# One program per engine for the front, the attention and the mix of a Hyena and attention encoder layer

## What is computed

```python
xn = rms_norm(x, norm1); proj = xn @ w_in            # -> hyena x0, x1, v | q | k | v
y_hy = hyena_mixer(...)      # width-3 conv; x0 * (long_filter * (x1 * v)) + skip, by Fourier transform
y_at = window_gqa(...)       # 8 heads of 64, 2 key heads, |q-k| <= 128, bias table, sink logit
mixed = concat([rms_norm(y_hy, hy_gain), rms_norm(y_at, at_gain)])
h = x + mixed @ w_out
y = h + (silu(gate) * up) @ w_down                   # gate, up = rms_norm(h) @ w_gate_up
```

## Time and profile before

| | us |
|---|---|
| three runs: median (lowest to highest) | 3209.15 (3200.5 to 3214.08) |
| the profiled execution: its time, its span | 3206.01, 3204.3 |
| TensorE busy | 2984.3 (93%) |
| VectorE, ScalarE, GpSimd busy | 1652.3 (52%), 1037.4 (32%), 358.5 (11%) |
| granted TensorE clock, mean over the span | 0.961 |
| front, up to TensorE's last product | 0 to 918.8 |
| front's end, bias rows, first loads of attention | 918.8 to 963.1 |
| attention | 963.1 to 1214.5 |
| loads of the mix, then the mix | 1214.5 to 1454.3 |
| feed-forward (first instruction) | 1463.65 to the end |

### The profile page before, as it was taken

The page is one execution under the profiler, slowest core; times in us unless marked ns, Lnnn a source line. Parts: engine busy times, 40 slices in busy tenths (PEclk is TensorE's granted clock), DMA queues, the critical chain, the costliest instruction groups (busy, mean ns, idle before and its releaser), DMA issues.

```text
span 3204.3 us, 41415 instructions
## 1 busy us (share of the span) xinstructions
PE 2984.3 (93%) x15240; PEld 2686.5 (84%) x15240; DVE 1652.3 (52%) x2394; ACT 1037.4 (32%) x1754; POOL 358.5 (11%) x411
## 2 busy tenths in 40 slices
PE   5988999898969997995999999899999989999998
PEld 4877889788956775885999999799999979999997
DVE  6765767685646886553343343433343344343343
ACT  4443544454525773213111211321111222121111
POOL 4322111232103550000000000000000000000000
PEclk9999999999986998997999999899999999999999
DMA  5466867765932224443221211321221232221220
GB/s 150 159 213 181 248 200 245 228 195 160 234 124 68 79 66 153 122 122 126 79 66 52 79 52 53 118 80 53 79 65 52 65 118 72 60 65 52 79 65 39
DMA packets 328861, 361.85 MB, mean 113 GB/s; under 512 B 39854, under 2 KB 269102, under 8 KB 328215
## 3 DMA queue, kind: packets, MB, share of 16 engines
q1 hardware_dynamic: 291032, 264.54, 29.3%
q0 software_dynamic: 37728, 95.96, 8.8%
HBM read 264.09 MB, written 83.12 MB: 108 GB/s over the span
## 4 chain that ended last, share of the span: by engine, by line
PE 51%; DMA 1%; DVE 1%; ACT 0%; issue 0%; SPq 0%; POOL 0%; POOLq 0%; DVEq 0%; ACTq 0%
PE ff_acc L81 12%; PE ff_acc L82 12%; PE ff_acc L83 12%; PE ff_down L81 6%; PE ff_down L83 6%; PE ff_down L82 6%; DMA ff_h<-h_dram 0%; DMA y<-ff_h 0%; DVE ff_xlo L2298 0%; DVE ff_xs L2287 0%; DMA ff_raw<-w_gate_up 0%; PE ff_down L2187 0%; ACT ff_xs L2242 0%; ACT ff_xhi L2248 0%; DVE ff_prod L2308 0%
## 5 line engine op out<-in xcount | busy, mean ns | idle before, releaser
L81 PE MATMUL ff_acc<-ff_xhi,ff_whi 128*128 128x384 f32 x2112 | 711.3, 337 | 16.3 <-DVE ff_xlo L2298 15.2
L82 PE MATMUL ff_acc<-ff_xlo,ff_whi 128*128 128x384 f32 x2112 | 709.7, 336 | 0.0
L83 PE MATMUL ff_acc<-ff_xhi,ff_wlo 128*128 128x384 f32 x2112 | 709.6, 336 | 0.0
L81 PEld LDWEIGHTS ff_acc<-ff_xhi,ff_whi 128*128 128x128 f32 x2112 | 399.8, 189 | 19.7 <-issue 13.8
L82 PEld LDWEIGHTS ff_acc<-ff_xlo,ff_whi 128*128 128x128 f32 x2112 | 399.9, 189 | 1.2
L83 PEld LDWEIGHTS ff_acc<-ff_xhi,ff_wlo 128*128 128x128 f32 x2112 | 399.4, 189 | 0.0
L2319 DVE TENSOR_TENSOR ff_h<-ff_h,ff_down 128x512 f32<-128x512 f32 x396 | 270.5, 687 | 228.1 <-PE ff_down L83 228.1
L2308 DVE TENSOR_TENSOR ff_prod<-ff_silu,ff_acc 128x384 f32<-128x384 f32 x132 | 73.2, 554 | 600.5 <-ACT ff_silu L2259 600.5
L81 PE MATMUL ff_down<-ff_dhi,ff_ahi 128*128 128x512 f32 x792 | 309.1, 390 | 7.3 <-DVE ff_alo L2311 7.3
L83 PE MATMUL ff_down<-ff_dhi,ff_alo 128*128 128x512 f32 x792 | 309.2, 390 | 0.0
L82 PE MATMUL ff_down<-ff_dlo,ff_ahi 128*128 128x512 f32 x792 | 309.1, 390 | 0.0
(11 more groups left out here) (261 smaller groups left out, 4925.9 us busy)
## 6 DMA issues: line engine op xcount, KB each, us to landing
ff_raw<-w_gate_up SPq DMA_DIRECT2D x134, 512.0 KB, 5.1
ff_draw<-w_down SPq DMA_DIRECT2D x33, 1024.0 KB, 5.1
pr_raw<-w_in SPq DMA_DIRECT2D x108, 256.0 KB, 5.5
pr_xs<-x SPq DMA_DIRECT2D x36, 512.0 KB, 4.6
f_dram<-fi_out POOLq DMA_DIRECT2D x32, 512.0 KB, 4.1
fs_a<-f_dram SPq DMA_DIRECT2D x32, 512.0 KB, 6.5
mo_x_in<-x SPq DMA_DIRECT2D x18, 512.0 KB, 4.2
h_dram<-mo_h POOLq DMA_DIRECT2D x18, 512.0 KB, 6.2
```

Source lines behind the costliest of these rows:

```text
L81: pe.matmul(out, still[0], moving[0], start=start, stop=False)
L82: pe.matmul(out, still[0], moving[1], start=False, stop=False)
L83: return pe.matmul(out, still[1], moving[0], start=False, stop=stop)
```

## The change

`front`, `bias_rows`, `attend` and `mix_out` become `front` and `mixers`. Each returns five functions, one per engine, and `build` opens one block in which each engine runs its part of the front and then its part of the mixers. In place of the barrier every engine first goes through `finished`, which waits for the front's last events (all stores landed too).

Moved into the front: k's high and low parts and v's transposes and parts (one stage `kvst`, stored to `k2_dram` and `v2_dram`, 6 pieces each), and the bias rows, in the steps `z_step`. 40 semaphores of the front are cleared by GpSimd at `z_step(4)` and given to the mixers. The others are cleared at the end of the block: 132 in all.

In the mixers block n has the attention of query block n, the preparation (turn of y, gate, norms) of tile n-1 and the mix matmuls of tile n-2, so there are 20 blocks. All is unrolled. There are two score banks instead of four. The probabilities aren't divided any more: the inverse sums are spread out by GpSimd, transposed by TensorE (`turn_denominators`, one bank in turn with the units and y), copied by ScalarE and multiplied into the finished output by GpSimd. The biased scores wait for one maximum per four heads instead of one per head. The w_out slices are loaded with two buffers in blocks 0 and 1.

The core of the diff (new lines, in the order of the file):

```diff
+    def finished(engine):
...
+        engine.wait_ge(handed_on, 1)
+        engine.wait_ge(unit_done, 2 * first_unit(ROUNDS))
+        engine.wait_ge(inverse_done, N2)
+        engine.wait_ge(hyena_out, 2 * NU + 2 * CT * NG)
...
+    def heads_at(n, i):
...
+        return ((0, 1), (2,), (3,), (4, 5), (6,), (7,))[i] if units(n) == 6 else ((0, 1), (2, 3), (4, 5), (6, 7))[i]
+    def mix_steps(n, i):
...
+        bounds = (0, 3, 6, 8, 11, 14, 16) if units(n) == 6 else (0, 4, 8, 12, 16)
+        return range(bounds[i], bounds[i + 1])
...
+        def bank(free_sem, free_at):
...
+            n = len(uses)
+            if n >= 2:
+                pe.wait_ge(*uses[n - 2])
+            uses.append((free_sem, free_at))
+            return n % 2
...
+            if 8 * n + h >= 2:
+                pe.wait_ge(biased, 8 * n + h - 1)
+            if h == 0 and n >= 3:
+                pe.wait_ge(rooted, n - 2)
...
+        for n in range(NB + 2):
+            for i in range(units(n)):
+                if n < NB:
+                    turn_unit(n, i)
+                if n + 1 < NB:
+                    for h in heads_at(n, i):
+                        score_head(n + 1, h)
+                if n <= NB and (n or i):
+                    before = (n, i - 1) if i else (n - 1, units(n - 1) - 1)
+                    if before[0] < NB:
+                        weigh_unit(*before)
+                if i == 0 and prepares(n):
+                    turn_y(n - 1)
+                if mixes(n):
+                    for step in mix_steps(n, i):
+                        mix_step(n - 2, step)
+                if i == units(n) - 1:
+                    if n < NB:
+                        turn_denominators(n)
+                    if prepares(n):
+                        sums(n - 1)
...
+    def scalar(act):
...
+        for n in range(NB + 2):
+            for i in range(units(n)):
+                if i == 0 and mixes(n):
+                    root(n - 2)
+                if n < NB:
+                    p_part(n, i)
+                    for m, h in raised_at(n, i):
+                        raise_head(m, h)
+                    if i == 1:
+                        sinks(n)
+                if i == 0 and 1 <= n <= NB:
+                    denominators(n - 1)
+                if i == 1 and 1 <= n <= NB:
+                    out_half(n - 1, 1)
+                if i == 2 and prepares(n):
+                    hyena_high(n - 1)
+                if i == late_unit(n) and prepares(n):
+                    attention_high(n - 1)
+                if n < NB and i == keys(n)[1] + 1:
+                    out_half(n, 0)
+                if i == units(n) - 1 and n + 2 < NB:
+                    q_part(n + 2)
...
+    def vector(dve):
...
+                if n < NB:
+                    p_part(n, i)
+                if i == 0 and mixes(n):
+                    invert(n - 2)
+                if mixes(n):
+                    for step in mix_steps(n, i):
+                        if step % 4 == 3:
+                            add(n - 2, step // 4)
+                if n + 1 < NB:
+                    for h in heads_at(n, i):
+                        bias_head(n + 1, h)
+                if i == 0 and prepares(n):
+                    gate(n - 1)
...
+                if i == units(n) - 1 and n + 2 < NB:
+                    q_part(n + 2)
```

More of the change, by code:

```diff
@@ new lines, in front @@
+    yhi = he.sb("yhi", [P, 2, 2, HY], F32R)
+    ylo = he.sb("ylo", [P, 2, 2, HY], F32R)
+    zo = he.sb("zo", [P, 2, 2, HY])
+    pinv = he.sb("pinv", [P, 2, 2, 2, LP], F32R)
+    ir = Place(nc, "ir", pr.end)
+    iz = ir.sb("z", [P, 2, 2, HY])
+    zhi = ir.sb("zhi", [P, 2, 2, HY], F32R)
+    zlo = ir.sb("zlo", [P, 2, 2, HY], F32R)
+    itab = ir.sb("table", [P, 2, 2, 2, P], F32R)
+    rows = ir.sb("rows", [P, 2, HY])
+    bias = ir.sb("bias", [P, HEADS, CH])
+    bias_end = ir.end
+    br = Place(nc, "br", fs.end)
@@ new lines, in front @@
+    brow = br.sb("table", [33, HEADS])
+    hot = br.sb("hot", [33, 512])
+    rel = br.sb("rows", [HEADS, 512])
+    fl = br.sb("fl", [P, P])
+    fallen = br.sb("fallen", [P, HEADS, CH])
+    kvst = Place(nc, "pr", ust_at).sb("kvst", [P, 2, CH], F32R)
+    held = Room(nc, early, "pr")
+    acc = held.ps("acc", [P, 2, 512])
+    turned = held.ps("turned", [P, 2, 512])
+    gen = held.ps("gen", [P, 4, 512])
+    gbc_in, ident_here, consts = r.sem("gbc_in"), r.sem("ident_here"), r.sem("consts")
@@ new lines, in front, with thirds, half_of, side @@
+    handed_on = y.sem("handed_on")
+    free_again = f.own + [*us_in, u_high, u_low, u_spectral, uo_re, uo_im]
+    mlp = gen[0:64, 0:3, 0:CH]
+    NJ = NOCT + 2
+    def thirds(tile64):
+        return tile64.rearrange("p (a c) -> p a c", a=3)
+    def half_of(tile64, half):
+        return tile64[:, HT * half:HT * half + HT]
+    def side(now, wave, wave_mid, wave_end, made_step, weigh_step, prompt, first_eighth, eighth,
+             first_u, u_step, product_step, return_step, first_z, z_step):
+        while now[0] < 2:
+            yield
+        wave(0, 0)
+        yield
+        wave_mid(0, 0)
+        wave(1, 0)
+        yield
+        wave_mid(1, 0)
+        wave_end(0, 0)
+        yield
+        wave(0, 1)
+        yield
+        wave_mid(0, 1)
+        yield
+        wave_end(1, 0)
+        wave(1, 1)
+        yield
+        wave_mid(1, 1)
+        wave_end(0, 1)
+        yield
+        for t in range(NTT + 1):
+            if t == 4:
+                wave_end(1, 1)
+            made_step(t)
@@ L417, in side @@
             yield
[L418 to L419 removed]
+            weigh_step(t)
             yield
[L421 removed]
+        for k in range(2):
+            prompt(k)
             yield
[L423 to L437 removed]
@@ L451, in side @@
[L451 to L465 removed]
+        while now[0] < 2 * NU + 3:
+            yield
+        first_u()
+        yield
@@ L2356, in build @@
+        r.own.extend(front_sems)
+        r.clear()
     w_gate_up = g["w_gate_up"].rearrange("(k p) c -> p k c", p=P)
```

3024 lines of the change are left out of this document (1501 added, 1523 removed).

## The result

The changed kernel takes 3246.3 us (median of four runs, 3243.6 to 3249.6) against 3211.6 us for the kernel before beside it; the ratio is **1.0127, interval 1.0105 to 1.0149**. It is slower, where the forecast had no difference that can be told (3222 us). The time lies inside the stated range, but the case that held is none of the rivals as written.

A forecast was written before the change was run, and what follows sets the result against it. TensorE's issue was taken to bound attention and mix. Last mix product +7.4, clears +6, one addition fewer -0.8: +12.6 us on the profiled 3206.0 gives 3219, or 3222 us as median (+0.4%); range 3184 to 3250.

The forecast's parts named there:

- blocks 0 and 1: First score to block 2, attention without mix at the slow clock: forecast 52.5 us (6.2 plus 46.3).
- the gap: Between the front's last product and attention's first score: 12 us, bounds 10 to 18.
- the ends: Blocks 15 to 19, up to the last mix product: 100.8 us.
- under the same 4.5: Block start: the scores' wait for q's low part is covered by y turning 4.5 us after unit 0's first issue.
- 28.5 us a block: Inner blocks 2 to 14: 26.1 us of TensorE issue plus stalls of 1.9 at y and 0.5 at head 5.
- a half clock that outlasts block 1: Rival, from block 2 on: the 0.50 clock lasts longer, 20 us more for one block, 3242 us; chance 0.12.
- "+6" at the last seam: Behind the last mix product: 132 semaphores cleared at once instead of 24, some 0.055 us each, 6 us more.
- the front's 9 us: Work moved into the front delays its last TensorE product by 9 us, between 3 and 20, to 927.8.
- The single stage: Front: waits of SP and ACT on the one k/v stage delay their other work; part of the 20 us upper bound.
- the new stalls at 47 us: Mixers: TensorE's new waits, at y and the scores among them, cost about 47 us in all.
- None of the stalls is 3222 - 47 = 3175: Rival, stalls at y and scores mostly covered: 3175 us with none, 3198 with half; chance 0.18.
- The dearer table switch (3244): Rival, unit 0's Exp switch: a second 1.4 us to clear the pipe, 16 times, 3244 us; chance 0.10.

The follow-up runs named there:

- e8: Changed kernel with ScalarE copying denominators before the exponentials and VectorE adding the next biases before the mix additions: 3193.5 us, 0.9947 times before.
- e9: Changed kernel with three thrown-away products issued before the turn of y in each of blocks 2 to 17: 3265.4 us, 1.0169 times before.
- e12: Changed kernel with three thrown-away products before the turn of y, and VectorE's next biases ahead of the mix additions: 3227.3 us, 1.0064 times before.
- e10: Changed kernel without the front's eight bias products on TensorE, VectorE writing zeros for the bias: 1.0107 times before.
- e7: Changed kernel with two staging tiles for keys and values, one per chunk, instead of one: 1.0099 times before.
- e1: Changed kernel with ScalarE copying the turned denominators before unit 0's Exp, nothing else: 3217.4 us, 1.0033 times before.
- e5: Changed kernel with the stores of h and the wait for the last two moved from GpSimd's to SyncE's queue: 3240.4 us, 1.0099 times before.

## Why the prediction was wrong

**What was right.** That both long stages are bound by TensorE's issue: the block without any wait is 26.0 us in e8, forecast 26.1. Near their forecasts were the gap (12, measured 13.5), blocks 0 and 1 (52.5, measured 50.7) with their slow clock, and the ends (100.8, measured 102.4). Right, too, were the queue that makes y late, link by link, and its time: 4.5 us behind the block's first issue, in both, and the block in which the clock holds, 28.4 for 28.5. Inside it the sum was split wrongly: the wait for q was put "under the same 4.5" and does lie under it, so that of the 1.9 us only 1.05 are idle at y itself and 0.60 at the score. e9 stumbled over just that.

**The step that failed: 28.5 us a block as the mean of blocks 2 to 14.** It priced idle time at its own length. It named the granted clock as a danger at the start, a half clock that outlasts block 1, and took it to be safe afterwards, because attention and mix had run at 1.00; but they had run nearly without waits (attention had one of 1.6 us at 1196.9, and kept its clock), and the change put some into every block. Thirteen blocks at 28.4 would be 369.2 us; the other 12.0 of the 12.6 us missed here are falls of the clock. That the falls hang on these waits is shown by e8 and e12 (no idle, no fall), not by e9, which filled one wait and kept another; why some blocks with a wait keep their clock stays open.

**The second: "+6" at the last seam, forecast 14.5 us, measured 22.1.** The clears were sized nearly rightly: 108 more at 0.064 us are 7.0, and moving 78 gave 5.0. So was the reading of the earlier trace rows: in the kernel before, the front's 106 clears run from 923.8 to 930.6. The step that failed is what the sum left out: it kept the rest of the seam as it had been and put GpSimd's own end at nothing new. Its DRAIN was 1.52 us behind the mix, and is 8.64 behind the one program, 7.1 more, which with the clears makes the miss. The kernel before had long ones too, 8.48 us at 901.2 and 5.1 at 1209.3, but the first was over before the front's last product and the second just before attention's last copy. What sets the length isn't shown; it was 1.5 us in the two stages in which GpSimd only issued stores (mix and feed-forward), and 5 to 9 where it had also computed.

**The third: the front's 9 us, measured 14.3.** The bias products (5.8) were right in size by the pace (4.9). The transposes of v (2.3) cost nothing that shows. The single stage, which stood in the bounds and not in the term, is one wait of 9.75 us, worth some 4 to 6. Some 3 us stay open, a unit that takes 15.0 instead of 12.2 us from 838 us on in the changed kernel, in e10 and in e7 alike.

**The rivals.** The forecast put the new stalls at 47 us; taking them out gave 58 (e8), the falls of the clock and the waits of the ends with them. "None of the stalls is 3222 - 47 = 3175" is some 3189 with the 5.3, 7.6 and 1.3 us missed elsewhere, and e8 has 3193.5. The dearer table switch (3244) and the late clock (3242) named nearly the measured time, by luck: neither happened, and the 3246.3 is the sum of three misses of one sign.

## What to carry to other kernels

When two stages are woven into one queue, an engine that was never late becomes late by its order: look for the instruction that the busiest engine waits for and ask what stands ahead of it that nobody waits for. Two swapped pairs of steps were worth 1.8% here, 58 us. Price a new wait of the matrix engine at more than its length as long as the clock is not shown to hold across it, and don't expect that filling one wait helps while another is left. At the end of a program, ask for each engine how much it still has to do behind its last wait, here 8.6 us of GpSimd, and let the last stores be issued by one that has little.

## What the runs showed of the hardware

The granted clock fell with TensorE 94% to 98% busy (359.57 of 381.20 us; 29.95 of 30.70). Waits of 0.6 us (e9) were followed by a fall in eight blocks running and by none in the next blocks with the same instructions, and by one in twelve blocks of e1; one fall lengthened a block by 1.3 us in the changed kernel and 1.5 in e9. With no wait it held for all of the 337.5 us (e8) and 340 us (e12) looked at. And GpSimd's DRAIN at the end of a block took 8.64 us in the changed kernel and 1.52 at the same place before; put ahead of the last store (e5), it cost nothing. One clear of a semaphore took 0.064 us.
